# Two output products of each later layer, split around the last attention heads

## What is computed

```python
for l in range(2):
    h = rms_norm_2(x, pre_norm[l]);  proj = h @ w_in[l]          # (256, 1024) @ (1024, 3072)
    oa = diff_attention(...)     # 6 heads D, normed, times silu(dgate)
    ob = gqa_attention(...)      # 6 heads G, times silu(ggate)
    om = softmax(mq @ mk^T) @ mv # 4 heads M, against a memory of 256 rows, times silu(mgate)
    y = concatenate([oa, ob, om]) @ w_out[l]                     # (256, 1024) @ (1024, 1024)
    x = x + rms_norm_2(y, post_norm[l])
```

## Time and profile before

| | us |
|---|---|
| median of three runs | 723.35 (722.22 to 725.70) |
| the profiled execution, device time | 722.24 |
| its span | 720.3 |
| PE busy | 657.8 (91%) |
| DVE busy | 353.1 (49%) |
| ACT busy | 332.3 (46%) |
| output products of layer 0 begin | 538.64 |
| output products of layer 1 begin | 691.07 |

### The profile page before, as it was taken

How to read it: one execution, slowest core, us unless ns; L and a number is a source line. 1 busy time by engine, 2 the same in 40 slices (tenths; PEclk the granted TensorE clock), 3 DMA queues, 4 the chain that set the end, 5 groups by cost and what they waited for, 6 DMA issues and landing times.

```text
span 720.3 us, 11852 instructions
## 1 busy us (share of the span) xinstructions
PE 657.8 (91%) x4637; PEld 515.9 (72%) x4638; DVE 353.1 (49%) x817; ACT 332.3 (46%) x780; POOL 43.7 (6%) x57
## 2 busy tenths in 40 slices
PE   6999999999899999999796999898979999889986
PEld 4977898789655365545262689877859899778876
DVE  1543656645630131011010557787775487887743
ACT  3465655551121022222020354777875547788642
POOL 6001000000000000000000322000000020100000
PEclk9999999999999999999898999999999999999999
DMA  9994335595999999999999847035353080081301
GB/s 286 328 308 149 116 117 176 193 347 211 353 357 415 411 414 409 415 411 414 414 410 407 262 165 243 1 116 178 112 181 117 6 288 1 28 266 60 117 1 59
DMA packets 94458, 166.80 MB, mean 232 GB/s; under 512 B 4287, under 2 KB 75745, under 8 KB 90305
## 3 DMA queue, kind: packets, MB, share of 16 engines
q1 hardware_dynamic: 92272, 160.88, 62.3%
q0 software_dynamic: 2000, 5.06, 2.1%
q10 hardware_dynamic: 128, 0.08, 0.0%
HBM read 164.92 MB, written 1.07 MB: 230 GB/s over the span
## 4 chain that ended last, share of the span: by engine, by line
PE 68%; DVE 10%; ACT 8%; SPq 7%; issue 3%; DMA 3%; DVEq 0%; ACTq 0%
PE psum L931 11%; PE psum L933 10%; PE psum L932 10%; SPq L795 6%; PE psum L1346 6%; PE psum L1302 6%; PE psum L974 4%; PE psum L1361 3%; PE psum L1329 3%; PE psum L1236 2%; DMA ring<-in_w_expert_up_dram 2%; PE psum L1066 2%; DVE w_low L2380 2%; PE psum L1283 2%; PE psum L1212 1%
## 5 line engine op out<-in xcount | busy, mean ns | idle before, releaser
L931 PE MATMUL psum<-a_high,w_high 128*128 128x256 f32 x512 | 150.1, 293 | 7.8 <-DVE w_low L2380 4.6
L932 PE MATMUL psum<-x_low,w_high 128*128 128x256 f32 x512 | 145.4, 284 | 0.0
L933 PE MATMUL psum<-a_high,w_low 128*128 128x256 f32 x512 | 145.4, 284 | 0.0
L931 PEld LDWEIGHTS psum<-a_high,w_high 128*128 128x128 f32 x512 | 98.6, 193 | 17.4 <-issue 6.8
L2380 DVE TENSOR_TENSOR w_low<-ring,w_high 128x1024 fp32r<-128x1024 f32 (+1 forms) x73 | 100.9, 1395 | 18.3 <-ACT w_high L1700 18.3
L1700 ACT ACTIVATE w_high<-ring 128x1024 fp32r<-128x1024 f32 (+1 forms) x79 | 96.1, 1220 | 10.7 <-DMA ring<-in_w_in_dram 7.3
L932 PEld LDWEIGHTS psum<-x_low,w_high 128*128 128x128 f32 x512 | 98.7, 193 | 0.1
L933 PEld LDWEIGHTS psum<-a_high,w_low 128*128 128x128 f32 x512 | 98.6, 193 | 0.0
L1346 PE MATMUL psum<-ring,q_c 128*32 128x512 f32 x320 | 58.7, 644 | 13.2 <-DMA ring<-in_w_expert_up_dram 7.2
L931 PE MATMUL psum<-w_high,a_high 128*128 128x256 f32 x240 | 68.8, 287 | 1.1 <-DVE mix_low L2391 1.0
L1302 PEld LDWEIGHTS psum<-tiles,x_nat 128*128 128x128 f32 x256 | 55.2, 307 | 7.0 <-issue 7.0
(11 more groups left out here) (347 smaller groups left out, 1190.7 us busy)
## 6 DMA issues: line engine op xcount, KB each, us to landing
ring<-in_w_in_dram SPq DMA_DIRECT2D x36, 1024.0 KB, 9.1
ring<-in_w_expert_down_dram SPq DMA_DIRECT2D x23, 1024.0 KB, 17.4
ring<-in_w_expert_gate_dram SPq DMA_DIRECT2D x40, 512.0 KB, 14.4
ring<-in_w_expert_up_dram SPq DMA_DIRECT2D x40, 512.0 KB, 15.0
ring<-in_w_out_dram SPq DMA_DIRECT2D x12, 1024.0 KB, 5.0
ring<-in_w_mem_kv_dram SPq DMA_DIRECT2D x4, 1024.0 KB, 11.9
xT<-in_w_expert_gate_dram SPq DMA_DIRECT2D x5, 512.0 KB, 11.2
xT<-in_w_expert_up_dram SPq DMA_DIRECT2D x5, 512.0 KB, 12.0
```

What stands on the lines that cost most here:

```text
L931: pe.matmul(dst, left[0], right[0], start=first, stop=False)
L932: pe.matmul(dst, left[0], right[1], start=False, stop=False)
L933: return pe.matmul(dst, left[1], right[0], start=False, stop=last)
```

## The change

In the later layers the mixed heads are split in three parts, (0,5), (5,7) and (7,8). Part 0 waits for G3 alone. ACT makes its high part in turn M1, right behind the `take` of the last tile; DVE its low part in turn M2, between `norms(M1)` and `maxes(M2)`. The first two output products, `y2 (l,0,0)` and `(l,0,1)`, are cut: PE runs their chunks 0 to 4 (15 matmuls each) ahead, the first at the opening of turn M3, the second in the first drain turn before `run_turn(M3)`, and leaves both groups open in banks 6 and 7. Chunks 5, 6 and 7 follow at the old place. Tiles 11 and 23 change places, so that the gate of chunk 2 is there in time.

```diff
-        tiles = [... [21], [23], [11], [], []]
+        tiles = [... [21], [11], [23], [], []]
+LAST_TILE = [job[2] for job in JOBS if job[0] == "tile2"][-1]
-MIX_PARTS = [[(4, 8), (0, 3), (3, 4)]] + [[(0, 7), (7, 8)]] * LAYERS
+MIX_PARTS = [[(4, 8), (0, 3), (3, 4)]] + [[(0, 5), (5, 7), (7, 8)]] * LAYERS
-    [("M", l, M_HEADS - 3), ("M", l, M_HEADS - 1)] for l in range(LAYERS)]
+    [("G", l, 3), ("M", l, M_HEADS - 3), ("M", l, M_HEADS - 1)] for l in range(LAYERS)]
 # PE
             def output_product(dst, job, phase):
                 order = [k for a, b in MIX_PARTS[phase] for k in range(a, b)]
                 waits = {a: mix_part(phase, n) for n, (a, b) in enumerate(MIX_PARTS[phase])}
-                return natural_product(dst, job, mix_low3, order, waits if job[-2:] == (0, 0) else {})
+                ahead = MIX_PARTS[phase][0][1] if phase and job[2] == 0 else 0
+                return natural_product(dst, job, mix_low3, order[ahead:], waits if job[-2:] == (0, 0) else {},
+                                       first=not ahead)
+            def output_ahead(job):
+                n, phase = JOB[job], job[1] + 1
+                if BY_DVE[n - 2]:
+                    pe.wait_ge(p_dve, taken(n - 2))
+                else:
+                    pe.wait_ge(p_act, taken(n - 2))
+                a, b = MIX_PARTS[phase][0]
+                natural_product(bank(6 + n % 2), job, mix_low3, range(a, b), {a: mix_part(phase, 0)}, last=False)
                     run_scores(step)
                     out_due = due_out(step)
+                    if what[0] == "M" and what[2] == M_HEADS - 1:
+                        output_ahead(("y2", what[1], 0, 0))
...
                         if OUT_OF[step - 1] != OUT_OF[step]:
                             run_out(OUT_OF[step - 1])
+                        if STEPS[step][0] == "M":
+                            output_ahead(("y2", STEPS[step][1], 0, 1))
                         run_turn(step)
 # ACT
+                    if job[0] == "tile2" and job[2] == LAST_TILE:
+                        mix_high(job[1] + 1, 0)
...
-                            mix_high(STEPS[step][1] + 1, 0)
+                            mix_high(STEPS[step][1] + 1, 1)
...
-                        mix_high(STEPS[step][1] + 1, 1)
+                        mix_high(STEPS[step][1] + 1, 2)
 # DVE
                         norms(step - 1)
+                    if what[0] == "M" and what[2] == M_HEADS - 2:
+                        mix_low_part(what[1] + 1, 0)
                     maxes(step)
...
-                    if STEPS[step][0] == "M":
-                        mix_low_part(STEPS[step][1] + 1, drained)
-                    else:
-                        mix_low_part(0, drained + 1)
+                    mix_low_part(STEPS[step][1] + 1 if STEPS[step][0] == "M" else 0, drained + 1)
```

More of the change, by code:

```diff
@@ L237, in schedule @@
                  + [("M", l, h) for h in range(M_HEADS)])
-        tiles = [[6, 7], [8, 15], [16, 12], [13], [14], [17, 9], [18], [20], [19], [10], [22], [21], [23], [11], [], []]
+        tiles = [[6, 7], [8, 15], [16, 12], [13], [14], [17, 9], [18], [20], [19], [10], [22], [21], [11], [23], [], []]
         before, behind = ([[] for _ in range(len(steps) + 2)] for _ in range(2))
@@ L944, in turned_product, with natural_product @@
                 return mm
-            def natural_product(dst, job, low, order, waits):
+            def natural_product(dst, job, low, order, waits, first=True, last=True):
                 pe.wait_ge(lows, SPLIT[job[:-1]] + 1)
@@ L954, in natural_product @@
                     mm = product(dst[:, 0:COLS], (a_high3[:, k, own], low[:, k, own]), [a[:, k, :] for a in w],
-                                 k == order[0], k == order[-1])
+                                 first and k == order[0], last and k == order[-1])
                 return mm
```

## The result

The changed kernel takes 717.75 us in the median of eight executions (716.54 to 719.21), the kernel before 722.86 in eight (719.90 to 726.18). The ratio is 0.992, with a 95% interval of 0.9899 to 0.9941. I had forecast 720.6 and a ratio of 0.996: the sign is right, the gain of 5.1 us is nearly twice the 2.8 of the sum.

What follows compares the result with a forecast made beforehand. The prediction took PE, busy 657.8 of 720.3 us, as the bound, with gains only from its waits. Gains of 0.74 and 2.03 us, 2.77 together, took 723.35 to 720.6 us (ratio 0.996); range 717.6 to 724.0.

Steps and rivals of the forecast that it cites:

- the 2.8 of the sum: Both later layers together: 0.74 us gained in layer 0 and 2.03 in layer 1, 2.77 us in all.
- all three stretches: PE's gap before layer 0's output, the products after it, and layer 1's gap: clock 1.00, no time lost.
- The idle time costs clock: Rival, chance 0.02: PE at half clock behind the gaps, 1.8 us a layer more to spare, 717.0 us.
- Gate and low pass on the chain of layer 0: DVE, turns M1 and M2: gate adds 0.45 us, part 0's low pass 1.41; maxima of M2 come 1.86 later.
- ACT's early high pass at no cost: ACT, turn M1 of layer 0: part 0's high pass costs nothing; without cover it would cost 1.27 us.
- Five chunks in a low pass: DVE: a low pass takes 0.265 us a chunk and 0.16 fixed, so five chunks take 1.49 us.
- Second piece ahead of the last transposes in layer 0: PE, first drain: the second product's early matmuls run to 537.6, so `run_turn(M3)` starts 0.47 us later.
- The bank stall: Layer 0: third output product waits for the first one's `take`, behind a weight slice's high pass on ACT; 0.55 us.
- Layer 1: covered as predicted: Layer 1: gate (0.45) and low pass (1.41) fit in DVE's 3.27 us wait, costing nothing; the layer gains 2.03 us.
- Hidden passes in layer 0: Rival, chance 0.18: `maxes(M2)` not on layer 0's chain, which gains 2.6 us; 4.6 with layer 1, 718.7 us.
- It gives nothing that shows: Rival, chance 0.17: 1.27 us more in layer 0 and half a us more in each layer; 0.5 remain, 722.9.
- the last head later by more than the products become shorter: Rival, chance 0.08: passes uncovered in either layer, second piece ahead of last transposes; `run_turn(M3)` +4.9 us, total 726.2 us.

Runs made afterwards that it cites:

- before again: The kernel before, unchanged, run once more as a control: median 724.02 us, ratio 1.0014.
- split only: The changed kernel without its work ahead; three parts, early passes and the exchange of tiles stay: median 724.57 us, ratio 1.003 to the kernel before.
- layer 1 alone: The kernel before with the change in the second of the two later layers only; layer 0 keeps its tiles, parts and order: median 722.01 us, ratio 0.9967.
- tile 20 filled: The kernel before with 8 matmuls that compute nothing before the product of tile 20, once a layer: median 725.37 us, ratio 1.0042.

## Why the prediction was wrong

**What bounds the kernel.** The step that failed is a term put at nothing, in this paragraph of the prediction: "The clock stands at 1.00 in all three stretches, so no time is lost to a lower one." That was read from one execution, and I carried it to the rival "The idle time costs clock" with a chance of 0.02. There are five traces of a layer 0 without work ahead (before, before again, split only, layer 1 alone, tile 20 filled). In four of them the clock falls ahead of the output products; it does so in none of the nine traces with work or filling there. The Trainium skill, "TensorE: Matmul & The Clock Gate", section "Part 1: The HAM clock gate (the "warmup" mystery)", has the rule that an idle array drops to half rate. The later traces agree with the drop (clock 0.50, 0.21 us a matmul), but PE was not idle throughout before it: it was busy for 2.24 of 4.00 us. My first trace was an execution without a fall in this place. The same trace had one at 494 us, outside the stretches that I had read.

**The sum.** Its steps held, and nearly all to 0.3 us. By the start of the third product I had 0.74 and 2.03 us; measured 1.08 and 2.32, in one trace of each kernel. In the list, "in the times of before" means with the difference between the first scores of M0 added, 2.45 us in layer 0 and 3.44 in layer 1.
- Gate and low pass on the chain of layer 0: maxima of M2 1.86 later; measured 1.87 (529.14 and 516.93 against 529.72 and 519.38).
- ACT's early high pass at no cost: it took 1.27 to 1.28 us, and DVE did not wait for it.
- Five chunks in a low pass: 1.49; measured 1.48. Two: 0.69; measured 0.69. High pass of two: 0.63; measured 0.64.
- Second piece ahead of the last transposes in layer 0: +0.47; measured 0.32, and the output of the last pair of heads started at 538.90 in the times of before, predicted 539.05.
- The bank stall: there, 0.29 us of waiting in the profile where I had 0.55; taking it away shortened layer 0 by 0.5 to the end (40.75). The third product started at 543.38 in the times of before, 0.28 before the 543.66 computed: 0.15 of it comes from the earlier last output, the rest from the evacuation and its handing-on. The other 0.06 of what layer 0 was better by is in the kernel before, whose third product started at 544.46 and not at 544.40; layer 1 has the same 0.06 (696.89, not 696.83).
- Layer 1: covered as predicted. The last transposes came 1.68 later (685.66 and the 3.44 make 689.10, against 687.42), predicted 1.83; the third product at 694.57 in the times of before, predicted 694.8.

**The missing term.** 1.6 us of clock in the mean, which the prediction had at zero; the steps were 0.5 us better than the sum to the end of the layers. My estimate for the rival was 1.8 us a layer more in every execution, 717.0 in all. A fall in fact cost 2.3 to 2.5 us in layer 0 (three traces against the first one) and 0.9 and 1.5 in layer 1 (two traces), but not every execution has one. That the result, 717.75, lies next to 717.0 is therefore partly luck: the price was too small in layer 0, and the number of falls too large.

**The rivals.** Hidden passes in layer 0: no, the maxima came as late as computed. "It gives nothing that shows" and the last head later by more than the products become shorter: no, the stages are shorter by 1.08 and 2.32 us. The control run and the 105 executions also say that the 3.5 us between three runs of the kernel before need not be taken as scatter alone: most of the spread between executions goes with the mean clock.

What stays open: why a given execution falls at a given wait. The two traces of the changed kernel have the same wait before tile 20 in layer 0, the second with a fall (clock 0.72 from 492 to 496 us) and the first without. The 0.9 us between the two first traces at 418 us, behind the expert stage, also were not taken apart; the changed kernel is ahead by 0.6 us already at 342 us and by 1.3 at 370, long before anything that the change touches, so they are no gain of the change.

## What to carry to other kernels

Where waits are followed by half clock, work moved into PE's waits pays twice: once for the work, and once for the matmuls behind the wait. So compare the mean clocks of many executions before you set that term to nothing from one trace. A split that makes a part available earlier can cost more than it gives by itself (1.1 us gained in layer 1, but ratio 1.003 in all here); it pays through what the bound engine does with it. When the work on the bound engine has moved, look again at the in-order queues beside it. Here a weight pass ahead of an evacuation, harmless before, and another ahead of the last maxima were together worth 1.6 us.

## What the runs showed of the hardware that I had not expected

- The granted clock of the same program differs between executions in waits of 1.8 to 2.0 us: 1.00 throughout in one, 0.50 for some 10 us in the next (531 to 541.2 us), and the mean clock of 49 of 105 executions of the kernel before is at 0.981 or below. Each 0.01 goes with 4.02 us.
- A fall came behind a stretch in which PE was not idle throughout: it was busy for 2.24 of the 4.00 us up to 530 us, and the clock fell at 531.
- One call of this float32 matmul, 128x128 by 128x256, shows as two matmul records 0.23 us apart, where one matmul of the three-pass products takes 0.12.
- With matmuls that compute nothing in a wait, no fall followed it in any trace taken (four traces with a filled wait before tile 20, two with filled waits ahead of the outputs). Before tile 20 of layer 0, seven of ten traces without filling have a fall, in layer 1 four of ten. The shortest filling, two calls or 0.93 us in a wait of 2.0 us, was seen in one trace only, in both layers.
